# Output gates of the second model's layer one projected ahead of the chunk loop, as seven half-size products, and fetched from memory chunk by chunk

## The reference, cut to what matters

```python
def hgrn2_mixer(h, lb, w_in, norm_g, w_out):
    q, f, i, g = jnp.split(h @ w_in, 4, axis=-1)      # h: 1024 x 1024, w_in: 1024 x 4096
    log_f = jnp.logaddexp(jnp.log(lb), jnp.log1p(-lb) + jax.nn.log_sigmoid(f))
    k = (1.0 - lb) * jax.nn.sigmoid(-f)
    qh = jax.nn.silu(heads(q)) * (HGRN_DK ** -0.5)
    o = gated_chunkwise(qh, k, heads(i), log_f)       # state carried over the tokens
    o = rms_norm(o, norm_g) * jax.nn.silu(heads(g))   # 8 heads of 128; g: the output gates
    return o.reshape(b, t, d) @ w_out

def moe_swiglu(h, w_router, ...):
    logits = (xt @ w_router).astype(jnp.float32)      # 1024 tokens x 8 experts
```

## Time and profile before

| | |
|---|---|
| time, median of 3 runs | 5410.61 us (5409.6 to 5414.27) |
| the profiled execution: its time | 5415.48 us |
| the profiled execution: its span, first to last instruction | 5413.3 us |
| TensorE matmul busy | 5242.6 us, 97% of the span |
| VectorE busy / ScalarE busy | 1595.9 us / 1027.7 us |
| mean granted TensorE clock | 0.982 of full speed |
| values' projection (L3116) starts | 2369.87 us |
| chunk 0's scores start | 2480.68 us |
| last chunk's `out` starts | 2885.43 us |

### The profile page before, as it was taken

How to read it: one execution, slowest core, us unless ns; L and a number is a source line. 1 busy time by engine, 2 the same in 40 slices (tenths; PEclk the granted TensorE clock), 3 DMA queues, 4 the chain that set the end, 5 groups by cost and what they waited for, 6 DMA issues and landing times. The chain is left out here.

```text
span 5413.3 us, 54717 instructions
## 1 busy us (share of the span) xinstructions
PE 5242.6 (97%) x21415; PEld 3655.6 (68%) x21415; DVE 1595.9 (29%) x2863; ACT 1027.7 (19%) x1823; POOL 67.4 (1%) x92
## 2 busy tenths in 40 slices
PE   8989999999999999999997999999999999999996
PEld 4445566755444444446765888888888888889995
DVE  3334446544333334624663010000001010101113
ACT  3511211233000000512442101101010111111111
POOL 0000000000000000000000000000000000000002
PEclk9999999999999999999997999999999999999998
DMA  5143033312111132541212454455546455555657
GB/s 194 39 177 128 20 107 107 143 42 65 51 47 46 49 134 93 150 138 68 90 67 90 140 156 154 141 170 167 159 139 173 152 159 167 163 175 152 188 155 253
DMA packets 687202, 678.03 MB, mean 125 GB/s; under 512 B 17431, under 2 KB 607306, under 8 KB 685002
## 3 DMA queue, kind: packets, MB, share of 16 engines
q1 hardware_dynamic: 664536, 623.44, 36.6%
q0 software_dynamic: 9680, 35.66, 1.8%
q10 hardware_dynamic: 12834, 16.82, 0.9%
HBM read 568.91 MB, written 106.96 MB: 125 GB/s over the span
## 5 line engine op out<-in xcount | busy, mean ns | idle before, releaser
L4040 PE MATMUL psum<-arena 128*128 128x272 f32 (+4 forms) x7168 | 1569.9, 382 | 6.7 <-issue 3.9
L4040 PEld LDWEIGHTS psum<-arena 128*128 128x128 f32 x7168 | 1363.1, 190 | 212.3 <-issue 8.7
L4056 PE MATMUL psum<-arena 128*128 128x272 f32 (+4 forms) x3584 | 795.2, 382 | 10.6 <-DMA arena<-in_moe_w_down 7.5
L4056 PEld LDWEIGHTS psum<-arena 128*128 128x128 f32 x3584 | 678.1, 190 | 109.9 <-DMA arena<-in_moe_w_down 7.7
L3922 DVE TENSOR_TENSOR arena<-arena,psum 128x512 f32 x224 | 154.1, 688 | 1423.1 <-ACT arena L3982 1423.1
L1386 PE MATMUL psum<-arena 128*128 128x512 f32 x1120 | 480.8, 592 | 0.0
L1386 PEld LDWEIGHTS psum<-arena 128*128 128x128 f32 x1120 | 212.8, 190 | 267.9 <-issue 267.9
L3982 ACT ACT_TABLE_LOAD x112 | 143.7, 1283 | 774.6 <-PE psum L4040 774.6
L1436 PE MATMUL psum<-arena 128*128 128x512 f32 x616 | 265.0, 592 | 0.0
L1935 PE MATMUL psum<-arena 128*128 128x256 f32 (+1 forms) x968 | 241.2, 409 | 1.9 <-PEq L99 1.9
L3982 ACT ACTIVATE arena<-psum 128x512 f32<-128x512 f32 x224 | 133.7, 597 | 573.7 <-PE psum L4040 572.5
(11 more groups left out here) (526 smaller groups left out, 4743.6 us busy)
## 6 DMA issues: line engine op xcount, KB each, us to landing
arena<-in_moe_w_gate SPq DMA_DIRECT2D x112, 1024.0 KB, 5.0
arena<-in_moe_w_up SPq DMA_DIRECT2D x112, 1024.0 KB, 7.5
arena<-in_moe_w_down SPq DMA_DIRECT2D x64, 1792.0 KB, 9.2
y_dram<-zeros SPq DMA_DIRECT2D x1, 22528.0 KB
x_dram<-arena SPq DMA_DIRECT2D x32, 512.0 KB, 3.1
arena<-in_ab_w_in SPq DMA_DIRECT2D x7, 2048.0 KB, 9.4
arena<-z_dram SPq DMA_DIRECT2D x8, 1664.0 KB, 7.7
arena<-in_c_w_in SPq DMA_DIRECT2D x6, 2048.0 KB, 13.0
```

The costliest lines, as they stand in the source:

```text
L4040: last = nc.tensor.matmul(g.ps[:, 2 * f + a, 0:N], wup[b][:, k, a * 256 + f * P:a * 256 + (f + 1) * P], xt[:, k, 0:N], start=(k == 0), sto ...
L4056: last = nc.tensor.matmul(g.ps[:, 4 + b, 0:N], wdn[b][:, k, :], hid[:, k, 0:N], start=(k == 0), stop=(k == EF_T - 1))
```

## The change

The gates leave the chunk loop. They are projected between the values and the loop, together with the values, in blocks of 512 columns (`n` = 0, 1 values, 2, 3 gates). A block takes the token tiles `t` and `t + 4` together and multiplies with seven products of half the depth (4 matmuls each) and half the width (256 columns) in place of eight, in the manner of Strassen and Winograd; VectorE makes four combinations of the weights for each block (`value_weights`) and adds the products up (`value_second`, `value_others`), ScalarE takes the first product and applies Silu to the gates, and SyncE stores them in a new `gate_dram`. In the loop a transfer of the chunk's gates takes the place of the transfer of its input `hc`. The transfers of the first two chunks stand partly behind the last product, since the buffers now hold operands of the products until then.

The logits change too: eight matmuls with 8 columns become eight with the router's weights as the stationary side, padded to 32 columns, whose results stand in four strips of 32 partitions (`logit_parts`); VectorE copies the strips (`take_parts`), and one more matmul adds them up (`logits`), one score later.

```diff
+            def value_product(n, t, j, stationary, moving):
+                i = 28 * n + nth(t, j)
...
+                for k in range(4):
+                    last = nc.tensor.matmul(g.ps[:, i % 8, 0:256], stationary[:, k, :], moving[:, k, :], start=(k == 0), stop=(k == 3))
+                last.then_inc(mm, 1)
...
+            for n in range(4):
+                pe.wait_ge((w_in + wg_in)[n], 16)
+                first_two(n, 0)
+                first_two(n, 1)
+                for t in range(4):
+                    if t >= 2:
+                        first_two(n, t)
+                    other_five(n, t)
+            pe.wait_ge(vtaken, 96)
             for c in range(NT + 2):
                 now, before, last_but = c < NT, 1 <= c <= NT, c >= 2
                 if now:
                     scores(c, 0)
                     scores(c, 1)
-                    gates(c, 0)
                     turn_keys(c)
                     scores(c, 2)
-                    gates(c, 1)
                     scores(c, 3)
                     keys_values(c)
...
                 if before:
                     turn_out(c - 1)
                 if now:
-                    gates(c, 2)
                     scores(c, 4)
                 if last_but and now:
                     turn_x(c - 2)
                 if now:
-                    gates(c, 3)
                     scores(c, 5)
...
-                    logits(c - 2)
+                    logit_parts(c - 2)
                 if now:
                     scores(c, 7)
+                if last_but and c <= NT:
+                    logits(c - 2)
...
+                for i in range(i0, i1):
+                    for j in range(4):
+                        last = nc.tensor.matmul(g.ps[32 * j:32 * j + 32, logit_bank(t), 0:P], wr[:, 4 * i + j, :], ht3[:, 4 * i + j, :], start=(i == 0), stop=(i == 1))
...
+            def value_weights(n):
+                wt = w_by_token[n]
+                dve.wait_ge((w_in + wg_in)[n], 16)
+                V.tensor_tensor(vt1, wt[:, 0:4, 256:512], wt[:, 0:4, 0:256], ALU.subtract)
+                dve.drain()
+                V.tensor_tensor(vt2, wt[:, 4:8, 256:512], vt1, ALU.subtract)
+                V.tensor_tensor(wt[:, 0:4, 256:512], wt[:, 4:8, 256:512], wt[:, 0:4, 256:512], ALU.subtract).then_inc(vt_made, 1)
+                dve.drain()
+                V.tensor_tensor(vt4, wt[:, 4:8, 0:256], vt2, ALU.subtract).then_inc(vt_made, 1)
...
+            def gate_silu(n, t):
+                for i in (1, 0):
+                    act.wait_ge(v_made, 8 * n + 2 * t + 2 - i)
+                    nc.scalar.activation(vacc[t % 2][i], vacc[t % 2][i], ACT.Silu).then_inc(gate_made, 1)
...
-                    for n in range(2):
-                        act.wait_ge(gg_done, 2 * c + n + 1)
-                        if c >= 2:
-                            act.wait_ge(og_made, c - 1)
-                        nc.scalar.activation(gate[c % 2][:, n * 512:(n + 1) * 512], g.ps[:, 6 + n, :], ACT.Silu).then_inc(gate_made, 1)
```

More of the change, by code:

```diff
@@ L3055, in logits @@
                     pe.wait_ge(lg_taken, t)
-                for k in range(k0, k1):
-                    last = nc.tensor.matmul(g.ps[:, logit_bank(t), 0:NE], ht3[:, k, :], wr[:, k, :], start=(k == 0), stop=(k == KD - 1))
-                if k1 == KD:
-                    last.then_inc(lg_done, 1)
+                for i in range(i0, i1):
+                    for j in range(4):
+                        last = nc.tensor.matmul(g.ps[32 * j:32 * j + 32, logit_bank(t), 0:P], wr[:, 4 * i + j, :], ht3[:, 4 * i + j, :], start=(i == 0), stop=(i == 1))
+                if i1 == 2:
+                    last.then_inc(lp_done, 1)
+            def logits(t):
+                pe.wait_ge(lp_taken, t + 1)
+                nc.tensor.matmul(g.ps[:, logit_bank(t), P:P + NE], partial, pick_sum, start=True, stop=True).then_inc(lg_done, 1)
             def out(c):
@@ L3105, in _ @@
                 product(n, 2, s4, rise[:, 4:8, :])
-            for n in range(2):
-                pe.wait_ge(w_in[n], 16)
-                for j in range(8):
-                    i = 8 * n + j
-                    if i < 8:
-                        pe.wait_ge(taken, 6 * (GROUPS - 1) if j < 4 else 6 * GROUPS)
-                    else:
-                        pe.wait_ge(v_taken, i - 7)
-                    for k in range(KD):
-                        last = nc.tensor.matmul(g.ps[:, j, :], ht[:, k, j * P:(j + 1) * P], wv[n][:, k, :], start=(k == 0), stop=(k == KD - 1))
-                    last.then_inc(mm, 1)
@@ L3382, in _, with value_second @@
-            last_decays(0)
-            for i in range(3, 6):
-                take_value(i)
-            state_queries(0)
-            for i in range(6, 16):
-                take_value(i)
+                return g.ps[:, i % 8, 0:256]
+            def value_second(n, t):
+                low, high = vacc[t % 2]
+                if n or t >= 2:
+                    dve.wait_ge(v_out[t % 2], 32 * (2 * n + t // 2))
+                else:
+                    dve.wait_ge(q_out[t], 16 * 4)
+                dve.drain()
+                dve.wait_ge(vfirsts, 4 * n + t + 1)
+                V.tensor_tensor(low[:, 0:256], vp1[t % 2], value_at(n, t, 1), ALU.add).then_inc(vtaken, 1)
@@ L3389, in _ @@
+            for n in range(4):
+                value_second(n, 0)
+                value_second(n, 1)
+                for t in range(4):
+                    if t >= 2:
+                        value_second(n, t)
+                    value_others(n, t)
+                    if n == 0 and t == 0:
+                        decays(0)
+                        last_decays(0)
+                    if n == 1 and t == 1:
+                        state_queries(0)
             dve.wait_ge(k_out, 16 * F)
```

200 lines of the change are left out of this document (140 added, 60 removed).

## The result

The changed kernel takes **5449.95 us** (median of 4 runs, 5446.04 to 5451.94) where the kernel before took 5410.1 beside it (4 runs, 5404.74 to 5414.27): a ratio of 1.0073, 95% interval 1.0057 to 1.0089, or +40 us. 5455 was predicted, in a range from 5425 to 5482. The profiled execution took 5446.04 us, its span is 5443.8.

The account below looks back on a forecast made before the run. It took TensorE to bound middle chunks, with VectorE's chain limiting once gates leave. Projection +83.5, chunk 0 -4, seven chunks -33.6 and ends -1.5 gave +44 on 5410.6: 5455 us, range 5425 to 5482.

Parts of the forecast that it names:

- The projection: Values and gates ahead of the loop: 896 instructions at 0.216 us, 193.5 us in place of 110.0, so +83.5 us.
- The waits: TensorE in a middle chunk waits for VectorE: 4.3 us before scores 3, 0.7 before scores 5, 1.2 before scores 6.
- The clock: The gap before scores 3 lowers TensorE's clock in every chunk, adding 3.5 us: chunks of 46.7, bounds 43.2 and 51.5.
- at full clock: Middle chunks if the clock never falls: 43.2 us each, +16 in all, 5427 us; as a rival, chance 0.13.
- rival of a second fall: Clock stays low or falls again at scores 5 and 6: 1.7 us more per chunk, +56 in all; chance 0.17.
- Chunk 0: First chunk, without gates or outputs: 44 us in place of 48.3, 4 less, bounds 36 to 48.
- The logits: Router logits in each chunk: strips 0.8 us plus sum 0.1 for 1.70; eight times, -6 us, from -12 to +2.
- The sum: Whole kernel: all terms together give +44 us, 5455 us from 5410.6; this likeliest case has 0.58.
- the seven chunks behind it: Chunks 1 to 7 at 46.7 us in place of 51.5: -33.6 us.
- the ends: Chunk 1 without `turn_x`, chunk 7 without decays, last two iterations changed by the logits only: -1.5 us.

Follow-up runs that it names:

- The gates left out: Kernel before without the gates' matmuls, their Silu and their input's transfer (gate constant 1): 5440.54 us, 1.0052; token routing differs, so only the loop can be compared.
- the filler: Changed kernel with four useless 512-wide matmuls between scores 2 and scores 3 of each chunk: 5422.92 us, 1.0033 to the kernel before.
- the half filler: Changed kernel with two useless 512-wide matmuls between scores 2 and scores 3 of each chunk: 5444.27 us, 1.0066 to the kernel before.
- the logits alone: Kernel before with only the logits changed to the new form: 5396.01 us, 0.9975 to the kernel before.
- the gates kept: Changed kernel with all gates projected in the chunk loop as before, its new values and logits unchanged: 5386.65 us, 0.9958 to the kernel before.
- one more matmul: Kernel before with one useless 8-column matmul added ahead of each token tile's logits: 5410.34 us, 0.9998 to the kernel before.
- the half gates: Changed kernel with the gates' second 512 columns back in the loop as two pieces per chunk: 5393.66 us, 0.9973 to the kernel before.

## Why the prediction was right

**The projection.** 193.5 us were predicted from layer zero's 0.216 us per instruction; it is 193.6 us, without a stall.

**The waits.** Predicted 4.3 us ahead of scores 3, 0.7 ahead of scores 5 and 1.2 ahead of scores 6; the trace after has 4.21, 0.45 and 1.00. What made this possible was that VectorE's chain up to queries(2) had no tie to the gates, so that its times in the trace before could be kept as they stood while TensorE's work ahead of them was added up anew. The gates left out show the same 4.21 us with nothing else of the change in place.

**The clock.** Queries(4) was put at 19.6 to 20.5, it starts at 19.7; the chunk at 46.7, chunks 3 to 5 take 46.8 to 47.6; at full clock 43.2, the filler shows 43.32. The evidence of chunk 0, that less than half of this wait had brought the clock down, pointed the right way: the clock fell in all of chunks 2 to 7, behind 4.21 us, and in the half filler in all six, behind 2.44. But it was weaker than the prediction took it. The same 1.98 us in the kernel with the logits alone, and 2.27 us with the gates kept, brought nothing down. The prediction also has the clock at its low level all through the 512-wide piece of 5.47 us; at half pace that piece would take twice its 3.6 us, so the clock came back within it.

The Trainium skill's rule (TensorE: Matmul & The Clock Gate, Part 1, on oscillation) is that bursts parted by idle stretches pay the return to the low clock in every turn. The trace agrees: the granted clock is 0.89 to 0.93 in each of chunks 2 to 6. The prediction's rival of a second fall happened in part: a piece behind scores 6 in chunk 5 takes 5.35 us for 3.65.

```profile
2816.41 1.97 PE L3008 MATMUL psum<-arena 128*128 128x64 f32 x16 [1.01 <-DVE arena L3230]
2818.22 5.35 PE L3034 MATMUL psum<-arena 128*128 128x512 f32 x8
```

A piece of 5.35 us stood in chunk 5 before the change too, 12 us later in the chunk, so this one may well not be the change's.

**Chunk 0.** Predicted 44 us, measured 44.1, and here two errors cancel. Behind `pick` 32 us of work at half pace and 4 us of waits were predicted; it is 29.3 us of work, since a part of the scores ran at full pace, and 6.1 us of waits (4.75 and 1.39). The clock is 0.66, and the scores run at half pace behind two waits:

```profile
2571.22 7.09 PE L3008 MATMUL psum<-arena 128*128 128x64 f32 x32 [5.70 <-DVE arena L3240]
...
2591.01 10.72 PE L3008 MATMUL psum<-arena 128*128 128x64 f32 x48 [4.75 <-DVE arena L3230]
```

**The logits.** 0.9 us were predicted for the new form and 0.76 measured (0.57 + 0.19) in place of 1.70. The strips' 16 instructions take 0.036 us each where L539 had 0.05 (by the last start in the earlier trace rows, 67.1 and not the 66.9 of the prediction, it is 0.05 too). The Trainium skill's figure for three column tiles (the same page, Part 3, measured speedup) is 2.38 times. The four strips here, with 128 columns, are 1.70 / 0.57 = 3.0 times as fast as the eight products in a row, more than that figure.

**The sum.** +44 were predicted, and the end of the stage moved by +42.0 in the profile: +81.9 to the loop's start (+83.5 predicted; 1.4 of the difference is the earlier start of the part), chunk 0 -4.2 (-4), the seven chunks behind it -36.7 (-33.6), the ends +1.0 (-1.5). What the sum didn't have is a term for the code behind the stage, where the profile after is 11.5 us shorter, 6.7 of them between router and experts; how much of this belongs to the change and how much to the two executions stays open. And the -4.2 of chunk 0 is as much the kernel before's: where the clock holds behind the 1.98 us, as with the logits alone, chunk 0 takes 44.9 us without the change's help. The nearness of the medians, +40 against +44, is therefore in part luck; the runs of each of the two kernels spread by 6 to 10 us.

**Where the expected gain of the change went.** Seven products in place of eight save an eighth of the gates' matmuls, but in the loop most of these matmuls covered waits and so cost little. In chunk 3 gates and logits took 14.7 us of work away. 5.66 us came back as waits. Another 4.4 us came back as busy time (41.17 us, where 51.49 - 14.7 = 36.8 were left): 3.6 of them are the half pace of scores 3, `keys_values` and the transposes, which matches the 3.5 us that the filler gave back in this chunk, and the remaining 0.8 isn't traced. So 4.65 us were gained, against 83.6 us / 8 = 10.4 us of projection per chunk.

## What to carry to other kernels

Before work is taken out of a loop, walk the loop without it: what the engine waits for then is read from the other engines' rows, and work that lay in another engine's chain is worth only what exceeds that chain. A wait of TensorE (here 4.2 us, and even 2.4) can cost a second time through its clock, here nearly as much as the wait itself, so the choice of what to move out is not all or none (two pieces out lost 7 us, four lost 63), and where the wait can't be removed, useless wide matmuls in it can pay. And compare small variants by the stage that they touch, not by the whole time alone: a wait elsewhere that comes and goes can be as large as their effect.

## What had not been expected of the hardware

- 2.44 us of idle time between wide and 64-wide matmuls brought the clock down in all six chunks of the half filler, 0.72 us did not in the full one. In the half filler's chunk 3, scores 3 still ran at full pace, and the fall hit the instructions 1.8 us behind the wait.
- In between, the length of the wait alone didn't decide. In chunk 0, 1.98 us brought the clock down in three profiles (two of the kernel before, and the one with one more matmul) and not with the logits alone, 2.27 us did not with the gates kept, and 1.00 us did in chunk 6 of the half gates.
- Adding 28 us of matmuls (8 x 3.49) to the changed kernel made its loop 20.5 us shorter and the kernel 27 us faster.
- The wait of some 5 us of `issue` within the first 24 transposes of the experts stands in both profiles of the kernel before and in none of those of the eight others that route the tokens alike. Its cause is open.
- The kernel with the filler has runs near 5422 and near 5435 us, at the same kernel. The first have a granted clock of 0.983 or 0.984, the others of 0.980 or 0.981, so the clock goes along with the difference; the place isn't known, since only one of the first was profiled.
